# Two attention orders of a two-block transformer kernel dealt anew, and a norm total issued five tiles earlier

## What is computed

```python
def first_block(x, ...):
    for layer in range(2):
        h = rmsnorm(x, attn_norm[layer])
        if layer == 0:
            qa, ka, va, qb, kb, vb, qi, ki, wi = split_cols(h @ w_in_even[0], sizes_even)
            mixed = concat(moba_attention(qa, ka, va), dsa_attention(qb, kb, vb, qi, rmsnorm(ki), wi))
        else:
            mixed = dilated_mixture(*split_cols(h @ w_in_odd[0], sizes_odd))
        x = x + mixed @ w_o[layer]
        x = x + conv_ffn(rmsnorm(x, ffn_norm[layer]), w_up[layer], ..., w_down[layer])
    return rmsnorm(x, final_norm)

def second_block(x, c, ctx, ...):
    h_lat = rms_norm(x, norm_mix) * (1.0 + m_lat[:, :, 1]) + m_lat[:, :, 0]
    h_ctx = rms_norm(ctx, norm_mix) * (1.0 + m_ctx[1]) + m_ctx[0]
    ... = features(h_lat, w_in, ...)      # h_lat @ w_in, split into queries, keys, values, gates
    ... = features(h_ctx, w_in, ...)
    ya, yb, yc = window_attn(...), global_attn(...), hgrn2_bidir(...)
    x = x + m_lat[:, :, 2] * merge_branches(ya, yb, yc, ...)
    x = x + m_lat[:, :, 5] * conv_ffn_2(...)
    return rms_norm(x, norm_final)
```

## Time and profile before

| | us |
|---|---|
| median of 3 runs | 2295.92 |
| profiled execution | 2296.61 |
| its span (first to last instruction) | 2294.8 |
| TensorE busy | 2281.1 |
| weight loads busy | 1885.7 |
| VectorE busy | 1438.1 |
| ScalarE busy | 1107.9 |
| GpSimd busy | 396.4 |

### The profile page before, as it was taken

The page is one execution under the profiler, slowest core; times in us unless marked ns, Lnnn a source line. Parts: engine busy times, 40 slices in busy tenths (PEclk is TensorE's granted clock), DMA queues, the critical chain, the costliest instruction groups (busy, mean ns, idle before and its releaser), DMA issues. The chain is left out here.

```text
span 2294.8 us, 30499 instructions
## 1 busy us (share of the span) xinstructions
PE 2281.1 (99%) x11966; PEld 1885.7 (82%) x11966; DVE 1438.1 (63%) x2318; ACT 1107.9 (48%) x1801; POOL 396.4 (17%) x297
## 2 busy tenths in 40 slices
PE   9999999999999999999999999999999999999998
PEld 8877788888888778888888878888888889888887
DVE  7898569858644666773676475557778335543543
ACT  6666654324434555442444366775555234432442
POOL 0013222202210001220222130001102122220222
PEclk9999999999999999999999999999999999999999
DMA  5222144433423223443343231011112432332231
GB/s 192 74 83 84 56 165 147 165 102 124 150 84 101 93 60 132 157 168 117 110 152 105 85 106 56 11 49 56 56 51 74 129 109 89 111 101 93 92 113 62
DMA packets 70222, 233.05 MB, mean 102 GB/s; under 512 B 8032, under 2 KB 10208, under 8 KB 69952
## 3 DMA queue, kind: packets, MB, share of 16 engines
q1 hardware_dynamic: 70080, 231.11, 30.3%
HBM read 224.18 MB, written 4.28 MB: 100 GB/s over the span
## 5 line engine op out<-in xcount | busy, mean ns | idle before, releaser
L487 PE MATMUL psum<-hH,wH 128*128 128x512 f32 (+1 forms) x1840 | 732.2, 398 | 0.6 <-DVE hL L641 0.3
L489 PE MATMUL psum<-hH,wL 128*128 128x512 f32 (+1 forms) x1840 | 714.6, 388 | 0.0
L488 PE MATMUL psum<-hL,wH 128*128 128x512 f32 (+1 forms) x1840 | 713.8, 388 | 0.0
L474 DVE TENSOR_TENSOR wL<-raw,wH 128x1024 fp32r<-128x1024 f32 (+2 forms) x353 | 446.3, 1264 | 362.1 <-ACT wH L469 361.0
L469 ACT ACTIVATE wH<-raw 128x1024 fp32r<-128x1024 f32 (+2 forms) x353 | 363.5, 1031 | 503.6 <-PE psum L489 476.7
L489 PEld LDWEIGHTS psum<-hH,wL 128*128 128x128 f32 x1840 | 345.3, 188 | 71.3
L487 PEld LDWEIGHTS psum<-hH,wH 128*128 128x128 f32 x1840 | 345.8, 188 | 70.6 <-issue 4.3
L488 PEld LDWEIGHTS psum<-hL,wH 128*128 128x128 f32 x1840 | 346.2, 188 | 61.3 <-issue 0.7
L2030 POOL TENSOR_TENSOR sg<-sg,cv 128x512 f32<-128x512 f32 x66 | 95.1, 1441 | 677.1 <-ACT sg L1857 677.1
L487 PE MATMUL psum<-gH,wH 128*128 128x512 f32 x506 | 197.0, 389 | 0.0
L489 PE MATMUL psum<-gH,wL 128*128 128x512 f32 x506 | 196.9, 389 | 0.0
(11 more groups left out here) (402 smaller groups left out, 3532.1 us busy)
## 6 DMA issues: line engine op xcount, KB each, us to landing
raw<-in_up SPq DMA_DIRECT2D x132, 512.0 KB, 3.2
raw<-in_dn SPq DMA_DIRECT2D x48, 704.0 KB, 4.0
raw<-in_win SPq DMA_DIRECT2D x56, 512.0 KB, 3.3
mbuf<-in_wmod SPq DMA_DIRECT2D x48, 512.0 KB, 3.3
raw<-in_we SPq DMA_DIRECT2D x33, 512.0 KB, 3.4
tm<-toep SPq DMA_DIRECT2D x32, 256.0 KB, 4.3
raw<-in_wo SPq DMA_DIRECT2D x32, 256.0 KB, 2.6
raw<-in_wq SPq DMA_DIRECT2D x16, 512.0 KB, 3.3
```

The source lines that it names most:

```text
L474: ve.do.tensor_tensor(flat_of(wLb, n), flat_of(rawb, n), flat_of(wHb, n).bitcast(F), ALU.subtract).then_inc(*w_lo.up(n))
L487: pe.do.matmul(o, H[:, k, :], high(k), start=k == 0, stop=False)
L488: pe.do.matmul(o, H[:, k, :], low(k), start=False, stop=False)
L489: ins = pe.do.matmul(o, L[:, k, :], high(k), start=False, stop=k == kt - 1)
```

## The change

The context total moves inside the second context unit, behind its tile k = 2. In C1 two more ticks stand ahead of the first step and two less behind the last. In E0 steps 6 and 7 go from (3, 3) to (4, 3) ticks and steps 32 and 33 from (2, 1) to (1, 1). No instruction is added or taken away.

```diff
         if a.layer == 1:
-            out_ = [("ticks", 64 + 20)]
+            out_ = [("ticks", 64 + 22)]
             per = [(2, 2)] * 28 + [(2, 1)] * 6 + [(0, 0)]
-            last = 10 + 32
+            last = 8 + 32
...
-            per = [(4, 3)] * 6 + [(3, 3)] * 18 + [(2, 2)] * 6 + [(2, 1)] * 4 + [(0, 0)]
+            per = [(4, 3)] * 8 + [(3, 3)] * 16 + [(2, 2)] * 6 + [(2, 1)] * 2 + [(1, 1)] * 2 + [(0, 0)]
...
             for k in range(KD):
                 pe_tile(pe, n, c_part(pe, bank[2 * i + 1][:, :CTX]), k)
-            if i == 1:
-                pe_end_sums(pe)
+                if (i, k) == (1, 2):
+                    pe_end_sums(pe)
```

## The result

| | before | after |
|---|---|---|
| median, us | 2295.91 (2295.74 to 2296.04, 6 runs) | 2304.80 (2302.56 to 2307.70, 6 runs) |
| profiled execution | 2296.61 | 2305.28 |
| its span | 2294.8 | 2303.5 |
| TensorE busy | 2281.1 | 2282.9 |

The ratio is 1.0039 [1.0027, 1.0051]: 8.9 us slower, where 2.3 us faster was forecast. It lies above the range of 2291.2 to 2296.2, and above the 2300.5 beyond which the prediction had put 0.02. The executions are also 5.1 us apart now, where these six of before are 0.3 us apart (in 30 others, beside the later runs, they are 1.7 apart).

A forecast was written before the change was run, and what follows sets the result against it. TensorE, busy 2281.1 of 2294.8 us, was taken as the bound, so only its waits could be won. Gains of 2.7 (block 2), 0.8 (E0) and 1.0 (C1) less 2.2 (C1) gave 2293.6; 8-in-10 range 2291.2 to 2296.2.

The forecast's parts named there:

- E0, what the shift does behind step 7: Behind E0's step 7, VectorE does one `wL` (1.2 us) earlier in some steps; no TensorE wait there, booked 0.
- E0, the end: E0's steps 32 and 33 give two ticks back; no wait there now, booked 0, with at worst 0.3 us lost.
- E0, the wait of step 7: TensorE's wait of 0.69 us (0.86 by starts) for scaled probabilities shrinks to 0 to 0.1; gain 0.8 us.
- C1, the cost: At C1's begin the bias loads go out late behind a weight load; second scores wait 2.0 us, 2.2 lost altogether.
- the rival with the half clock: The clock drops behind C1's wait at a price of 1.6 us: 0.7 gained, 2295.2; chance 0.2.
- C1, the gain: Scores in C1's last and five middle pairs stop waiting for the keys' low part; gain taken as 1.0 us.
- Block 2: At block 2's begin the total and its `hL` chain start 1.80 us earlier, clock held; gain 2.7 us.
- The slots: TensorE's successive work on each `hL` in block 2: slot 1 waits 0.2 us, slot 2 0.8, none from slot 4.
- The sum: Over the whole kernel, 2.7 + 0.8 + 1.0 - 2.2 = 2.3 us less.
- the slower one: C1's steps 0 to 3 stay late and the clock halves once: 5.9 us against gains of 4.5, 2297.3; chance 0.08.

## Why the prediction was wrong, step by step

- **E0, what the shift does behind step 7: the step that failed.** The text says of VectorE's `wL`, one operation earlier in the row: "no wait of TensorE stands there now, and I book 0". Two things were missing. The waits of before say where slack is used up, not how much is left elsewhere. And I followed the shift on VectorE alone, against TensorE's next need of `wL`, not to the next engine in the chain. The runs show the chain add (late by L474), exponentials, L469, L1495, next scores, and 4.5 us of waits at the scores of four pairs; at the first of them it runs from the row at 142.73 to the row at 147.04. L1495 as a gate of the next pair's scores appears nowhere in the prediction. The whole term, booked as 0.8 gained, measured 7.3 lost.
- **E0, the end.** Booked 0 with 0.3 as the worst. There were 2.8 us of waits. The run with the end alone has none of them, and 1.9 of them stand ahead of the shortened steps. Wrong in size and, for those 1.9 at least, in cause.
- **E0, the wait of step 7.** Right: it went, in the change and in every run with the longer steps.
- **C1, the cost.** Right in every link: the load held by `wL`, the tile behind the weight load (5.3 us forecast, 5.0 seen), the wait at the second scores (2.0 forecast, 1.79 and 2.10 seen). The fit that the Trainium skill gives (DMA: Bandwidth & Descriptors, Anatomy of one DMA) is for transfers that GpSimd issues, and these are SyncE's. The estimate from it made the tiles 1.5 us earlier, and so the wait about 0.5; the trace did not agree. The term is 2.2 in the sum. With the clock held the late tiles cost 2.6 us (C1's stretch 2.27 longer than before without early loads and 0.36 shorter with them), and in medians 3.0 + 0.6 = 3.6. The 1.0 between the two would be the rival with the half clock, which had 0.2, in part of the executions; none of those was profiled, so that stays open.
- **C1, the gain.** 1.0 was taken, the `kLr` waits did go, but 0.56 came back as a wait of one of the last transposes for VectorE's scaling. 0.4 net in the trace with early loads, 0.6 in the medians.
- **Block 2.** The slots came as laid out, 0.2 and 0.7 of wait by starts where 0.2 and 0.8 were forecast. The size was off by a slip of accounts: 0.9 of the 2.7 was half clock, and that was in the profiled execution, 0.7 us longer than the median. Subtracted from the median of 2295.92, which by its length did not hold it, it counted as a gain that was not there to be had. The end of E0 alone shows this: profiled with before's waits and the clock held in block 2, it took 2295.91, and its begin of block 2 is 0.8 shorter than before's. 1.9 was to be had, and 1.9 was measured.
- **The sum.** Forecast -2.3. With the terms as measured alone: -1.9 + 3.0 + 7.3 = +8.4. The whole measured +8.9. E0's term is 8.1 off, C1's (net 1.2 lost) 1.8, block 2's 0.8. No rival had E0 as its place: the slower one stood in C1, with 2297.3. The range was too narrow for the same reason. It was made from the bounds of the steps that I had looked at.

## What to carry to other kernels

When a table deals filling against a chain on several engines that run in order, one tick more does not shift the filling evenly: it flips which of two neighbours comes first, and where the chain has no slack a flip can cost the whole long operation (here 1.0 to 1.4 us). Not every flip does: of the first five places here one cost nothing, and at three of the other four undoing one of the two flips was enough. Compare the two orders on every engine over the whole stretch in which the phase differs, and for each flip follow the late result through the next engine's queue to TensorE, also through the release of a bank. A gain that is half clock in the profiled execution belongs to that execution, not to the median.

## What the runs showed of the chip that was not expected

- Waits of nearly one length at one place had different effects on the clock. 1.79 us in C1 was followed by 0.50, 2.10 us at the same place was followed by 1.00. In E0 1.84 us was followed by 0.50 in the profile after and by 1.00 in the run of E0's table alone. The begin of block 2 with the total in its old place was profiled in ten kernels, in all of them behind waits of 1.06 to 1.07 and 0.48 to 0.49: the clock stood at 0.50 behind them in four (before, E0's table alone, `wL` one tick later, `wH` two ticks later) and held in six. The Trainium skill (TensorE: Matmul & The Clock Gate, section HAM oscillation) says that waits can let the clock be throttled, in an example whose waits are longer than any here; the runs agree that it can, and show that it need not.

The begin of block 2 with the clock held, from the end of E0 alone, against the earlier trace rows:

```profile
1276.00:1279.40 3.40, 2.92 (x12) 1.94 (x13) 3.33 (x5) 1.45 (x2) 0.00 (x0) 1.00 0.00 0
```

- The scatter fits this, but is not explained by it alone. Over 11 runs each, the three kernels with the early total and no new wait in C1's begin or E0 spread over 0.8 to 0.9 us; the others without C1's late tiles and with at most one long wait in the middle of E0 spread over 1.3 to 1.7; C1's ticks alone spread over 3.7. E0's table alone spread over 3.0 in 7 runs, with `wL` one tick later over 2.4 in 8, and the change over 5.1 in 6. In the change the two fastest executions have a mean granted clock of 0.999 and the slowest 0.997. A long wait can cost more than its length, and a single profile of such a kernel does not tell its median. Before itself spreads over 1.7 in 30 runs on one chip and over 2.4 in 33 on another.
